# A four-stage edit of a hybrid decoder step: head boundaries, page loads of the last head, and the norm and the end of a convolution layer

## The reference, cut to what matters

```python
def rmsnorm(x, g):
    return x * rsqrt(mean(x * x, -1) + EPS) * g

def mixer_ab(h, ...):                                  # layer 0
    rq, rk, rv, rg, sq, sk, sv = split(h @ w_in)
    o = retention(rotary(rq), rotary(rk), rv)          # prompt in chunks of 128, samples from a state
    ret = silu(rg) * head_layernorm(o, gn_g)
    sb = sb_attend(sq, sk, sv)                         # prompt: its own keys; samples: 8 pages of 128 each
    return concat(ret, sb) @ w_out

def conformer_conv(h, buf, w1, b1, dw, dwb, ln_g, ln_b, w2, b2):   # layer 1, h = rmsnorm(x, g_mix)
    a, gt = split(h @ w1 + b1, 2)
    u = a * sigmoid(gt)
    c = layernorm(depthwise_conv(concat(buf, u), dw) + dwb, ln_g, ln_b)   # 31 taps per channel
    return silu(c) @ w2 + b2, last 30 columns
```

## Time and profile before

| | |
|---|---|
| runs (median of 3) | 3377.71 us (3373.37 to 3384.82) |
| profiled execution | 3373.28 us, its span 3371.4 us |
| TensorE busy | 3184.4 us, 94% of the span |
| VectorE, ScalarE, GpSimd busy | 1892.9, 764.0, 789.1 us |
| chain of waits | TensorE 85%, VectorE 10%, DMA 2%, ScalarE 2% |
| mean granted TensorE clock | 0.975 of full speed |

### The profile page before, as it was taken

One profiled execution on the slowest core, in us unless ns is written; L12 is line 12 of the kernel. 1 busy time (PEld: TensorE's weight loads), 2 busy tenths in 40 slices (PEclk: granted clock), 3 DMA queues, 4 the chain that ended last, 5 costly groups with the idle time before them and its releaser, 6 DMA issues.

```text
span 3371.4 us, 45117 instructions
## 1 busy us (share of the span) xinstructions
PE 3184.4 (94%) x19144; PEld 2952.0 (88%) x19144; DVE 1892.9 (56%) x2808; ACT 764.0 (23%) x1093; POOL 789.1 (23%) x424
## 2 busy tenths in 40 slices
PE   7999897699999999999997999799999999999996
PEld 6778887599579999999997887599679999999996
DVE  5655677451436545554557799751446645555456
ACT  4766222210122111111112222420122211111111
POOL 2111121032013323333322002023003333233231
PEclk9999998799999999999998999899999999999998
DMA  3111444423501111111112101021701111111111
GB/s 134 38 52 49 139 145 133 157 69 116 240 19 49 45 50 44 49 47 44 50 45 50 38 28 36 14 76 52 311 13 49 51 44 45 50 45 47 48 44 70
DMA packets 83644, 238.16 MB, mean 71 GB/s; under 512 B 15723, under 2 KB 20715, under 8 KB 81651
## 3 DMA queue, kind: packets, MB, share of 16 engines
q1 hardware_dynamic: 74962, 217.96, 19.5%
q10 hardware_dynamic: 8480, 17.32, 1.4%
HBM read 217.93 MB, written 17.32 MB: 70 GB/s over the span
## 4 chain that ended last, share of the span: by engine, by line
PE 85%; DVE 10%; DMA 2%; ACT 2%; issue 1%; SPq 0%; DVEq 0%; ACTq 0%
PE ps L450 69%; PE ps L919 2%; PE ps L837 2%; PE ps L760 2%; PE ps L748 2%; PE ps L814 1%; DVE tls L1334 1%; DVE X L1326 1%; PE ps L582 1%; DVE t L1326 1%; PE ps L552 1%; DVE junk L1559 1%; DVE Gl L1326 1%; PE ps L515 1%; DMA pg<-in_cv 1%
## 5 line engine op out<-in xcount | busy, mean ns | idle before, releaser
L450 PE MATMUL ps<-Hh,Wh 128*128 128x344 f32 x3552 | 779.3, 328 | 55.2 <-DVE Hl L1326 30.9
L422 POOL CAST Wh<-wraw 128x1024 fp32r<-128x1024 f32 x210 | 232.1, 1105 | 2516.7 <-PE ps L450 2461.1
L450 PE MATMUL ps<-Hl,Wh 128*128 128x344 f32 x3552 | 760.2, 323 | 0.0
L450 PE MATMUL ps<-Hh,Wl 128*128 128x344 f32 x3552 | 756.5, 322 | 0.0
L450 PEld LDWEIGHTS ps<-Hh,Wh 128*128 128x128 f32 x3552 | 603.6, 190 | 81.6 <-issue 50.0
L450 PEld LDWEIGHTS ps<-Hl,Wh 128*128 128x128 f32 x3552 | 606.9, 191 | 0.0
L450 PEld LDWEIGHTS ps<-Hh,Wl 128*128 128x128 f32 x3552 | 598.4, 190 | 0.0
L424 POOL TENSOR_TENSOR Wl<-wraw,Wh 128x1024 fp32r<-128x1024 f32 x210 | 557.0, 2652 | 16.8
L1326 DVE TENSOR_TENSOR X<-ps,X 128x1032 f32<-128x1032 f32 x200 | 244.4, 1230 | 296.6 <-PE ps L450 296.6
L1326 DVE TENSOR_TENSOR ub<-ps,rst_d 128x1032 f32<-128x1032 f32 x88 | 108.5, 1233 | 419.1 <-PE ps L450 236.3
L961 ACT ACTIVATE cb<-ub,fp 128x1032 f32<-128x1032 f32 x88 | 110.1, 1252 | 968.5 <-DVE ub L1326 968.5
(11 more groups left out here) (254 smaller groups left out, 3359.3 us busy)
## 6 DMA issues: line engine op xcount, KB each, us to landing
wraw<-in_wts SPq DMA_DIRECT2D x224, 512.0 KB, 3.5
pg<-in_ck SPq DMA_DIRECT2D x64, 256.0 KB, 2.7
pg<-in_cv SPq DMA_DIRECT2D x64, 256.0 KB, 2.7
cc<-in_cmk SPq DMA_DIRECT2D x16, 1024.0 KB, 10.0
cc<-in_cmv SPq DMA_DIRECT2D x16, 1024.0 KB, 9.7
mwa<-in_memw SPq DMA_DIRECT2D x16, 512.0 KB, 7.7
mwb<-in_memw SPq DMA_DIRECT2D x16, 512.0 KB, 7.7
X<-in_x SPq DMA_DIRECT2D x6, 1032.0 KB, 6.6
```

The costliest lines, as they stand in the source:

```text
L422: pool.tensor_copy(Wh[:, j, :], wraw[:, j, :]).then_inc(w_hi, 1)
L450: ins = mm(o, w[:, wcol[0], wcol[1]:wcol[1] + P], r, start=first and a == 0, stop=last and a == 2)
```

## The change

- Stick-breaking heads: the barrier between the pairs goes. A head starts with the scores of units 0 and 1 on TensorE and VectorE, and the turned values come behind them.
- Last retention head: its 16 key pages and 16 value pages are loaded to an area of their own (`pgl`, on the rows of `Hh` and `Hl`), the keys as soon as the last projection tile is done, the values behind the state's load. There is no wait for a free slot. Of the reciprocal of the head norm, two thirds are moved ahead of the running sums over pages.
- Norm 3 is deferred: the end of the FFN of layer 0 splits `X` (`high_of_x`, `low_of_x`), TensorE doesn't wait at the barrier there, and `gate` becomes two multiplications of the accumulators by the norm's factor and, further on, a third instruction with the sigmoid (`gated` on VectorE).
- Convolution's end: the gate of the last chunk comes ahead of the `cd` taps of the chunk before; the last chunk has 16 diagonals on TensorE (`dg`, `dgx`) and no `cd` taps; the column sums of chunks 0 to 5 stand ahead of its joint taps; GpSimd waits until the mean is subtracted before it splits the tiles of `w2`.

```diff
-        DEFERRED = (0, 1, 2, 4, 5)
+        DEFERRED = (0, 1, 2, 3, 4, 5)
+        rt["pgl"], _ = place("pgl", [P, 4 * PG, H * P], F32, x_at + 4 * KC * N)
-            return dn["rst_d"][:, :] if nk else rst0
+            return {0: rst0, 3: con[:, C_HEAD:C_HEAD + N]}.get(nk, dn["rst_d"][:, :])
...
+            def last_pages(m):
+                for n in (2 * m, 2 * m + 1):
+                    page = sp.value_load(rt["pt"][0:1, bass.ds(2 * PG * (H - 1) + n % (2 * PG), 1)], min_val=0,
+                                         max_val=NPAGES - 1)
+                    load(rt["pgl"][:, n:n + 1, :], (cache_k, cache_v)[m // 8][bass.ds(page, 1)]
+                         .rearrange("a p n -> p a n"), ss((LAST_K + LAST_V)[m]))
...
+                if not more:
+                    sp.wait_ge(tile_done, T_OUT)
+                    for m in range(8):
+                        last_pages(m)
                 ended(sp, i + E_SB)
                 load(rt["s0"][:, :, :], stret[bass.ds(i, 1)].rearrange("h d b e -> d (h b) e"), ss("ld_s0"))
+                if not more:
+                    for m in range(8, 16):
+                        last_pages(m)
+                    return
...
+            pool.wait_ge(ss("l_d"), KC)
             for i in range(T_W2 // 2, NT // 2):
...
                     scores(0)
                     scores(1)
+                    turned_values()
...
-                end_stage(pe, end_pe, i + 1)
+            end_stage(pe, end_pe, E_SB)
...
-                end_stage(pe, end_pe, e1)
+                pe.drain().then_inc(end_pe, 1)
+                if l:
+                    ended(pe, e1)
...
-            norm_sum(3)
-            for s in range(2):
-                pe.wait_ge(set_free[s], F_W1 + 1)
-            first_pair(T_W1, split_ready(3))
+            first_pair(T_W1, split_ready(3), F_W1, HA, 3)
...
+            pe.wait_ge(set_free[0], F_W1 + KC + 1)
+            for c in range(KC - 2):
+                channel_sums(c)
+            joint_taps(KC - 1)
+            channel_sums(KC - 2)
+            ins = channel_sums(KC - 1)
...
+                    dve.wait_ge(ss("r_root"), 2 * i + 1)
+                    for g in range(2):
+                        r = rt["rst"][:, g * GN:(g + 1) * GN]
+                        dve.reciprocal(r, r)
                     page_sums()
...
+                def finished(c):
+                    if l:
+                        sum_square(nk + 1, c)
+                    else:
+                        low_of_x(c, nk + 1, PCOL["g_mix"] + KC, HA)
...
             def gate(c, j):
-                dve.wait_ge(set_free[1], c + (F_W1 + 2))
-                stt(uu[:, j, :, W_OD:UP].rearrange("p e (g n) -> p g n e", g=GRP),
-                    pset(0).rearrange("p g (n e) -> p g n e", e=2), cpar[:, j, 0:1],
-                    grp(cf["sg"][:, :]).rearrange("p g (n e) -> p g n e", e=2), ALU.add, ALU.mult, set_free[0])
+                planes = uu[:, j, :, W_OD:UP].rearrange("p e (g n) -> p g n e", g=GRP)
+                dve.wait_ge(tile_done, T_W1 + 2 * c + 2)
+                if c == 0:
+                    dve.wait_ge(ss("n_rc"), n_at[3] + 3)
+                tt_(grp(cf["sg"][:, :]), pset(1), grp(rst_of(3)), ALU.mult, set_free[1])
+                tt_(planes, pset(0).rearrange("p g (n e) -> p g n e", e=2),
+                    grp(rst_of(3)).rearrange("p g (n e) -> p g n e", e=2), ALU.mult, set_free[0])
+
+            def gated(c, j):
+                planes = uu[:, j, :, W_OD:UP].rearrange("p e n -> p n e")
+                dve.wait_ge(set_free[0], c + (F_W1 + 2))
+                dve.wait_ge(ss("c_gate"), 2 * c + 1)
+                stt(planes, planes, cpar[:, j, 0:1], cf["sg"][:, :].rearrange("p (n e) -> p n e", e=2),
+                    ALU.add, ALU.mult, ss("c_gate"))
...
+                if c + 2 == KC:
+                    gate(c + 1, 1 - j)
-                for n in range(W_PE, W_EV):
+                for n in range(W_PE, W_EV if more else W_PE):
```

More of the change, by code:

```diff
@@ L196, in build @@
                             ("dg", [P, W_PE, P])], scr)
+        cf["dgx"], _ = place("dgx", [P, W_EV - W_PE, P], F32, where["sg"])
         ln, _ = layout([("lsq", [P, 2, N]), ("lrst", [P, N])], where["uu"])
@@ L256, in of_layer @@
         def of_layer(l, name, n):
-            return ss(name), n + l * COUNTS[name]
+            return ss(name), n + l * COUNTS[name] + BEFORE.get(name, 0)
+        LAST_K = [f"ld_cc_{m // 2}" for m in range(8)]
+        LAST_V = [f"ld_cc_{4 + m // 4}" for m in range(8)]
+        BEFORE = {**{s: 64 for s in LAST_K}, **{s: 128 for s in LAST_V}}
         def ended(e, n):
@@ L928, in _, with channel_sums @@
                 joint_taps(c - 1)
-            joint_taps(KC - 1)
-            for c in range(KC):
-                if c == KC - 1:
-                    pe.wait_ge(ss("c_ch"), 2 * KC + 1)
+            def channel_sums(c):
+                pe.wait_ge(ss("c_ch"), 2 * c + 3)
                 for g in range(GRP):
@@ L1263, in _ @@
             ffn(0, E_FF0, 2, T_FFN0, F_FF0)
-            norm(3)
+            roots(3)
             def conv_hi(t, j):
@@ L1291, in _ @@
                         a = CFP + n if n < W_OD else 2 + W_CONV
-                        fn(cf["dg"][:, n, :], ident, ACT.Identity, ss("c_dg") if n == W_PE - 1 else None,
-                           scale=cf["cpar"][:, j, a:a + 1])
+                        fn(cf["dg"][:, n, :], ident, ACT.Identity,
+                           ss("c_dg") if n == W_PE - 1 and c + 1 < KC else None, scale=cf["cpar"][:, j, a:a + 1])
+            for n in range(W_PE, W_EV):
+                a = CFP + n if n < W_OD else 2 + W_CONV
+                fn(cf["dgx"][:, n - W_PE, :], ident, ACT.Identity, ss("c_dg") if n == W_EV - 1 else None,
+                   scale=cf["cpar"][:, 1, a:a + 1])
             end_stage(act, end_act, E_FF0 + 1)
@@ L1439, in _, with turned_values @@
                         "p (a n) -> p a n", a=1), None)
-                    dve.wait_ge(ss("sb_vt"), h + 1)
-                    for j in range(2):
-                        copy(sb["svt"][:, 4 * j:4 * j + 4, :], ps[:, 6 + j, :].rearrange(
-                            "p (c n) -> p c n", c=4), ss("sb_vev"))
+                    def turned_values():
+                        dve.wait_ge(ss("sb_vt"), h + 1)
+                        for j in range(2):
+                            copy(sb["svt"][:, 4 * j:4 * j + 4, :], ps[:, 6 + j, :].rearrange(
+                                "p (c n) -> p c n", c=4), ss("sb_vev"))
                     def score(u):
@@ L1957, in _ @@
             gate(0, 0)
+            gated(0, 0)
             conv_lo(T_W1 + 3, 1)
```

116 lines of the change are left out of this document (69 added, 47 removed).

## The result

The changed kernel takes 3332.28 us (median of 4 runs, 3330.36 to 3336.65) against 3377.59 us before (4 runs, 3373.37 to 3384.82): a ratio of 0.9865, 95% interval 0.9846 to 0.9885. The forecast was 3334. The profiled execution took 3332.01 us, 41.3 us less than that of before; the sum said 39.6. The medians are 45.3 us apart: the forecast took the profiled execution of before, 3373.28 us, as its base, and all four runs of before in this comparison are slower than that.

A forecast was written before the change was run, and what follows sets the result against it. TensorE was taken as the bound, busy 94% of the span with 85% of the chain of waits. Terms -7.5 - 9.6 - 20.5 + 2 - 4 = -39.6 us led from 3373.3 to 3334 us, range 3320 to 3350.

The forecast's parts named there:

- the sum: Whole kernel: heads -7.5, last retention head -9.6, FFN's end and gate -20.5, loop +2, convolution's end -4, together -39.6 us.
- The term: Stick-breaking heads: scores first gain 2.0 us at each of three boundaries, 1.5 at the first head; 7.5 us, bounds 4 and 9.
- the bound of 10.5: Last retention head: upper bound of the gain from pages without waits, taken as 9.6 us, bounds 5 and 10.5.
- eight pairs in a row are 1.89 + 6 x 1.0: Last retention head: eight page-value pairs without waits take 7.9 us, ending at 623.4, so 9.6 us go.
- The first pair's end: Convolution's first pair of tiles after the FFN: ends at 1846.6 us, where before it ended at 1866.3.
- the wait at the gate: After the convolution's first pair: TensorE waits 3.3 us for two multiplications, against 4.58 for sigmoid and gate.
- no idle time over 3 us: Sign in the profile after: TensorE has no longer idle time between the FFN and the convolution's second pair.
- ScalarE's first taps: Convolution loop: they start only when a round starts, costed at nothing beside VectorE's small instructions; if not, 0.3 us a round.
- the late gate: Convolution's end: VectorE has 0.75 + 2.0 us to finish the sixth chunk and third gate instruction, within its 26.0 us.
- Moving GpSimd's splits: Convolution's end: two splits placed behind the subtraction cost nothing, or 2 us if they met the normalisation.
- heads keep nothing: Rival, stick-breaking heads: 1 us left per boundary, or the pages land late; 3341 us, chance 0.12.
- a round of 35 us: Convolution loop: a round above 35 us would prove the forecast wrong; rounds of 33.0 to 33.6 were expected.

The follow-up runs named there:

- the two slots: Changed kernel with the last retention head's sixteen page pairs loaded into the two page slots again, as in the other heads; 3348.79 us.
- the dense multiply: Changed kernel with the gate's second multiply writing in natural order into the chunk's output row, only the last instruction writing the two planes; 3329.37 us.

## Why the prediction was right

**Heads.** The mechanism is shown from both sides: undoing the order costs 9.6 us, putting the barrier back 0.8, where the prediction had the barrier at nothing. The term was too small: I took 2.0 us for each boundary out of 1.0 to 2.3, since two of VectorE's copies were only moved; measured is 5.75 - 3.38 = 2.37. Nothing of the copies came back.

**Last retention head.** -12.1 for -9.6, beyond the bound of 10.5. The failed step is "eight pairs in a row are 1.89 + 6 x 1.0": without waits a pair takes 0.70 us, not 1.0, and the eight 5.62 instead of 7.9. The 0.70 is a mean over two levels of the clock. From 610 to 614 the granted clock is 0.50 and 76 of the matmuls keep TensorE busy for 3.86 us; from 614 to 616 it is 0.96 and 60 take 1.76. Before, and with the two slots, the clock is 0.50 all through the page values. At the first rate all 128 would take 6.5 us, an estimate; so some 0.9 us of the surplus is a rise of the clock, which the prediction did not foresee. The start of the page values did not move, as said, and the split reciprocal is worth 1.6 us only because the values became so early.

**FFN's end and gate.** The first pair's end, with 22.56 us added (by so much the FFN is earlier), is 1846.3 (forecast 1846.6), the resumption 1849.5 (1849.9), VectorE's last sum of squares 1830.1 (1830.6), the wait at the gate 3.16 (3.3). Ahead of the sums of squares TensorE waits only 0.78 us and not 2.5: it came there 1.3 us later than reckoned, and VectorE was done 0.4 us sooner. The end is VectorE's, so it did not move by this. (The prediction's sign "no idle time over 3 us" there was at odds with its own 3.3.)

**Loop.** VectorE has become the bound of the convolution, by 33.50 against 33.03 us. The scattered multiply costs 1.94 and the third instruction 2.10; 2.0 and 1.9 were taken from the old gate. The experiments show that leaving out one tap, or the scatter of the multiply, brings the round back to TensorE's 33.03. ScalarE's first taps, which the prediction put at nothing because small instructions cover them, cost nothing indeed: VectorE waits 0.36 us for them only where two of these are taken away.

**Convolution's end.** -3.7 for -4.0; by the experiment the new gate with the old end would have been 2.4 us worse than before (34.3 against 31.95), which the sum did not have. It charged the late gate to VectorE, where it is hidden, and not to ScalarE's diagonals. Moving GpSimd's splits was put at nothing; setting GpSimd free again cost the stretch 1.3 us.

So the sum's 39.6 came near the 41.3 partly by cancelling: the five stages gained 43.6 us, 4.0 more than forecast, and unchanged stages, which the sum holds at nothing, gave back 2.3. That 3334 lies within 2 us of the measured median is luck in part too: from the median of before, 3377.59, the same sum leads to 3338 (from the medians of before beside the experiments, to 3334 to 3339). The rivals that would have shown (heads keep nothing, a round of 35 us) did not occur.

## What to carry over

A barrier was not what the boundary cost: the first instruction behind it on the engine that everything waits for was, so look at what that engine does first, and put there what releases the others. When a wait for transfers goes, price the instructions behind it by their own rate in a dense run and not by rows that were paced by the wait; the clock of that run may be another one as well. After such a gain read the round of every engine again: here VectorE, which had 2.62 us to spare in a round, became the next bound by 0.5 us, and the output pattern of one instruction (0.72 us) made the difference.

## What the runs showed of the hardware

- Writing one row of 1032 f32 columns into two planes of even and odd columns cost VectorE 1.94 us, in natural order 1.22. A three-operand instruction from SBUF into the planes takes 2.10 us whether its input is scattered or dense.
- A GpSimd subtraction of 2.4 to 2.7 us lengthened VectorE's work on operands in SBUF by 2.1 to 2.6 us in an addition of squares (3.43 for 1.22), a low part (3.43 for 1.28) and three short taps (4.95 for 2.33). It did not do so everywhere: an addition that reads an accumulator took 1.23 us beside one (X, at 1774.09 in the changed kernel), as without.
- After 1.98 us without work at 1790 TensorE's clock fell in the changed kernel's first profile (granted clock 0.79 from 1790 to 1798; three products take 1.06 us at the lower level, 1.2 GHz, and 0.64 at 2.4 GHz). In the profile with the dense multiply it stayed at 1.00 behind the same wait and fell behind the next one, of 2.33 us (0.76 from 1805 to 1812). The stretch from reciprocal to reciprocal over the FFN is 764.9 us there, 762.6 in the first.
- 128 small matmuls took 5.62 us at a mean granted clock of 0.65: at 0.50 first, 76 of them in 3.86 us, then at 0.96, 60 in 1.76 (8 count in both). Sixteen alone, at 0.50, are a row of 1.03 us.
- The time of a cross-attention went with its granted clock: over 80 us of it 1.00, 0.98, 0.96 and 0.94 came with 322.0, 323.7 to 324.5, 326.5 to 327.1 and 327.2 to 328.4 us.
